# Attention heads and gated-linear-attention chunks moved between the quarters of their projections, in two stages of a four-layer kernel

## The chip, the cores and the metric

One core of one Trainium2 chip runs the whole program. The metric is device time in microseconds (us), as a median over runs. The engines are named as in the profile: PE is TensorE's matmul, PEld its weight load, DVE is VectorE, ACT is ScalarE, POOL is GpSimd, SP is the engine that issues nearly all loads.

## The reference, cut to what matters

A sequence of 256 tokens, 1024 wide, passes through two blocks of two layers each. The change touches the mixers of the first block:

```python
mkv = (mem @ w_mem_kv[l]).reshape(B, MEM_LEN, 2, MEM_HEADS, MEM_HEAD_DIM)
# layer 0: gated linear attention (GLA), 4 heads, chunks of 64 tokens
h = x @ a_w_in[0]                     # q, k (4x96), v, r (4x192), gate root (16), qm (4x64)
g_pre = h[..., A_G0:A_G1] @ a_w_gate2[0] + a_b_gate[0]
log_a = log_sigmoid(g_pre) / 16
o = _gla(q, k, v, log_a)              # chunks: masked q k^T v, and a state carried from chunk to chunk
o = o * rsqrt(mean(square(o), -1) + 1e-6) * a_norm_g[0]
mix = silu(r) * o
# layer 1: dilated attention, 6 slots of 128, three groups of queries on the same keys and values
mix = _dilated_attention(qd, shared_k, shared_v)
# both: attention of 4 heads to 256 memory rows, then the output product and the layer norm
mo = _mem_attn(qm, mkv[:, :, 0], mkv[:, :, 1])
x = _layer_norm(DN_ALPHA * x + concatenate([mix, mo]) @ w_out[l], ...)
f = _peer(x, ...)                     # 128 x 128 experts, the long part of each layer
```

The three dilated groups are softmaxes weighted by their own sums, which is one softmax over the three masked score rows side by side; its numerators are added over the groups before they meet the values.

## The kernel before

**Projections.** `project_all` runs a list of projections on every engine. Each has two units (the two halves of the 1024 input rows, g = 0 and 1), and unit i of the list is projection i // 2, half i % 2. SP loads a unit in two halves into a ring of 7 buffers. ACT rounds a half (`round_half`), DVE subtracts to get the rest (`rest_half`), and TensorE multiplies three times per product (`mm3`): high by high, high by rest, rest by high. In a unit with g = 0, TensorE goes input chunk by input chunk over all outputs of the projection; with g = 1 it finishes one output after the other. After each quarter `project_pe` calls `beside(unit, quarter)`; ACT and DVE call it in `project_all` after rounding each half of the next unit. At the end of an odd unit `project_out` copies the outputs out of PSUM, in turn on DVE and ACT, and then `hooks` for that unit run. A projection's outputs lie in banks 0 to 3 or 4 to 7 in turn (`base` None), or from a given `base`. At g = 0 TensorE takes the banks of all outputs before its first matmul: `take` waits until the last reader of the bank is done, `give` names that reader.

**Heads.** Attention is a list of jobs, one for a head and 128 tokens. In step s, job s gets its scores on TensorE, job s - 1 its row maximum on DVE (`add_max` with the mask), job s - 2 its exponentials on ACT, job s - 3 is turned on TensorE, job s - 4 is copied from PSUM (even jobs on DVE, odd ones on ACT), job s - 5 meets its values on TensorE and job s - 6 is scaled and stored by DVE. All three engines walk the same steps, each in its own order. Before the change these steps run by themselves, after all projections (`join` waits for every engine), with their banks dealt out in turn over seven (`bank_plan`), and with filler matmuls between them (`busy`, tile `gk`, bank 7). For the dilated jobs (scores 384 wide for tokens 0 to 127, 768 for the rest) POOL adds the second and third group to the first (`heads_pool`), and TensorE turns the sum.

**First layer.** After seven projections (Aq, Ak, Ag, Av, Aw, Ar, As) with the gate's chain of small operations in hooks come eight memory jobs, then the chunks: products inside the chunks (`intra`), turned keys (`kend`), three states, the rows (`gla`, 128 tokens each), the head norms with one root for each 128 tokens, then `out_turn` and `out_pe` of the output product in four quarters of 256 input columns.

**Dilated layer.** After ten projections come twelve dilated and eight memory jobs, and then the output product.

**The same arrangement elsewhere.** The last attention stage ("stick") already has its steps between the quarters of its projections, with the projections in banks 0 to 3 and the steps in banks 4 to 7, and its last steps between the halves of the output product.

## Time and profile before

| | us |
|---|---|
| runs shown | 2862.23, 2867.27, 2860.39 (median 2862.23) |
| profiled execution, its own time | 2862.17 |
| its span, first to last instruction | 2860.2 |
| mean granted TensorE clock | 0.982 of full |
| first layer, first projection matmul to end of output product | 47.91 to 184.53 |
| dilated layer, end of projections to end of output product | 1115.50 to 1178.23 |

The program is one long chain of stages on one core. Busy shares over the whole span say little of a stage; the stretch that matters is read by windows and by the timeline. In a timeline row the number in brackets is idle time of that engine before the row. A matmul's record is longer than the pace at which matmuls follow each other, so paces are taken from start to start. A plain fp32 matmul leaves two records, which the xcount includes.

### The profile page before, as it was taken

The page shows a single profiled execution, that of the slowest core. Times are in us where ns is not written, and L with a number is a line of the kernel's source. Part 1 is how long each engine was busy: PE and PEld are TensorE (multiplying, and loading weights), DVE is VectorE, ACT ScalarE, POOL GpSimd, SP SyncE. Part 2 cuts the span into 40 slices and gives each one's busy share as a digit, 9 for nine tenths or more (in the row PEclk, how much of TensorE's full clock was granted, in tenths as well). Part 3 has the DMA queues.
Part 4 walks back from the last instruction along what each step waited for, and adds up shares of the span by engine and source line. Part 5 has one row for each costly group of instructions (what it writes and reads, how often), then busy time and mean ns, then how long its engine had stood idle before and what let it go on. Part 6 is the DMA issues. An engine that isn't in the chain of part 4 may idle for free.

```text
span 2860.2 us, 43908 instructions
## 1 busy us (share of the span) xinstructions
PE 2742.7 (96%) x17298; PEld 2407.5 (84%) x17298; DVE 2001.6 (70%) x3889; ACT 1345.8 (47%) x2188; POOL 302.5 (11%) x162
## 2 busy tenths in 40 slices
PE   7999999999999999999999999999999899898997
PEld 7779999998888888799999988888777678786776
DVE  4676988985555655679889755556657759656588
ACT  3423554444445534435454444455235357453465
POOL 0003950000000001049400000000110000000000
PEclk9999999999999999999999999999999999999999
DMA  5344554555665644445544555656421359532586
GB/s 191 113 136 126 177 175 157 155 164 184 195 194 191 223 147 133 142 133 177 170 157 157 167 185 195 194 192 210 125 89 24 125 193 355 185 99 68 174 296 226
DMA packets 175116, 479.04 MB, mean 167 GB/s; under 512 B 27184, under 2 KB 43456, under 8 KB 174912
## 3 DMA queue, kind: packets, MB, share of 16 engines
q1 hardware_dynamic: 171808, 473.29, 50.5%
q10 hardware_dynamic: 3104, 2.95, 0.3%
q8 instruction: 138, 2.26, 0.3%
q14 instruction: 66, 0.54, 0.1%
HBM read 474.61 MB, written 1.57 MB: 166 GB/s over the span
## 4 chain that ended last, share of the span: by engine, by line
PE 87%; DVE 7%; ACT 3%; POOL 2%; issue 1%; DMA 0%; SPq 0%; DVEq 0%; ACTq 0%; POOLq 0%
PE ps L134 86%; POOL ring_rest L154 2%; PE ps L137 2%; DVE spl L154 1%; DVE big L162 1%; ACT big L140 1%; DVE st L178 1%; ACT whi L140 1%; DVE big L154 1%; DVE xb L162 1%; DVE st L162 0%; ACT spl L140 0%; DVE xr L154 0%; POOL big L154 0%; DVE grouped L154 0%
## 5 line engine op out<-in xcount | busy, mean ns | idle before, releaser
L140 ACT ACTIVATE whi<-ring 128x1024 fp32r<-128x1024 f32 x512 | 542.5, 1060 | 686.6 <-PE ps L134 684.7
L134 PE MATMUL ps<-xr,whi 128*128 128x256 f32 x4096 | 750.4, 285 | 11.1 <-POOL ring_rest L154 10.7
L154 DVE TENSOR_TENSOR ring_rest<-ring,whi 128x1024 fp32r<-128x1024 f32 x412 | 503.5, 1222 | 318.1 <-ACT whi L140 318.1
L134 PEld LDWEIGHTS ps<-xr,whi 128*128 128x128 f32 x4096 | 640.4, 193 | 14.0 <-DVE big L184 8.6
L134 PE MATMUL ps<-whi,Ar 128*128 128x512 f32 x2048 | 631.1, 389 | 4.5 <-DVE Ar L154 4.5
L134 PE MATMUL ps<-xr,ring_rest 128*128 128x256 f32 x2048 | 580.8, 284 | 0.0
L154 DVE TENSOR_TENSOR spl<-ring,spl 128x1024 fp32r<-128x1024 f32 (+3 forms) x384 | 435.3, 1163 | 124.9 <-ACT spl L140 115.8
L134 PEld LDWEIGHTS ps<-whi,Ar 128*128 128x128 f32 x2048 | 384.5, 188 | 84.4 <-DVE Ar L154 4.9
L140 ACT ACTIVATE spl<-ring 128x1024 fp32r<-128x1024 f32 (+3 forms) x384 | 373.4, 1008 | 94.5 <-PE ps L134 75.6
L134 PE MATMUL ps<-ring_rest,Ar 128*128 128x512 f32 x1024 | 398.4, 389 | 0.0
L134 PEld LDWEIGHTS ps<-xr,ring_rest 128*128 128x128 f32 x2048 | 394.4, 193 | 0.0
L140 ACT ACTIVATE big<-ps 128x256 f32<-128x256 f32 (+25 forms) x417 | 153.6, 368 | 366.0 <-PE ps L134 249.8
L154 POOL TENSOR_TENSOR ring_rest<-ring,whi 128x1024 fp32r<-128x1024 f32 x100 | 267.2, 2689 | 263.4 <-ACT whi L140 262.8
L134 PE MATMUL ps<-xr,spl 128*128 128x256 f32 (+2 forms) x2184 | 276.6, 287 | 14.3 <-DVE xr L154 9.7
L134 PEld LDWEIGHTS ps<-xr,spl 128*128 128x128 f32 (+2 forms) x2184 | 267.3, 190 | 19.3 <-DVE xr L154 12.4
L134 PE MATMUL ps<-spl,xr 128*128 128x512 f32 (+2 forms) x1152 | 250.5, 375 | 10.4 <-DVE xr L154 5.3
L134 PEld LDWEIGHTS ps<-spl,xr 128*128 128x128 f32 x1152 | 203.1, 196 | 48.2 <-DVE spl L154 6.4
L134 PE MATMUL ps<-spl,grouped 128*128 128x512 f32 x960 | 234.1, 400 | 4.9 <-DVE spl L154 4.4
L134 PEld LDWEIGHTS ps<-ring_rest,Ar 128*128 128x128 f32 x1024 | 192.3, 188 | 40.0
L134 PEld LDWEIGHTS ps<-spl,grouped 128*128 128x128 f32 x960 | 180.1, 191 | 43.7 <-DVE spl L154 5.4
L154 DVE TENSOR_TENSOR big<-big 128x8 f32<-128x8 f32 (+18 forms) x145 | 158.6, 1125 | 5.8 <-POOL big L154 3.7
L151 DVE COPY big<-ps 128x256 f32<-128x256 f32 (+7 forms) x134 | 55.8, 421 | 147.4 <-PE ps L134 141.0
(127 smaller groups left out, 2488.6 us busy)
## 6 DMA issues: line engine op xcount, KB each, us to landing
ring<-in_peer_u_dram SPq DMA_DIRECT2D x256, 512.0 KB, 3.5
ring<-in_peer_v_dram SPq DMA_DIRECT2D x256, 512.0 KB, 3.5
ring<-in_moe_gate_up_dram SPq DMA_DIRECT2D x128, 512.0 KB, 5.0
ring<-in_moe_w_down_dram SPq DMA_DIRECT2D x64, 512.0 KB, 5.1
ring<-in_peer_w_q_dram SPq DMA_DIRECT2D x32, 512.0 KB, 4.6
ring<-in_sb_w_in_dram SPq DMA_DIRECT2D x24, 512.0 KB, 4.8
ring<-in_ab_w_in_dram SPq DMA_DIRECT2D x20, 512.0 KB, 6.0
ring<-in_w_out_dram SPq DMA_DIRECT2D x16, 512.0 KB, 4.7
```

The lines of the kernel that those rows point to most:

```text
L134: return self.e.matmul(o, l, r, start=start, stop=stop)
L137: return self.e.transpose(o, i, ident)
L140: return self.e.activation(o, i, f, **k)
L151: return self.e.tensor_copy(o, i)
L154: return self.e.tensor_tensor(o, a, b, op)
L162: return self.e.scalar_tensor_tensor(out=o, in0=a, scalar=s, in1=b, op0=op0, op1=op1)
L178: return self.e.bn_stats(o, i)
```

## The change

The steps of the heads become functions of their own (`heads_step_pe`, `_dve`, `_act`) and run in `beside` between quarters of the projections: 14 steps in units 3 to 9 of the first layer, and 20 of 26 steps in units 4 to 17 of the dilated one, the other six between the halves of its output product (`dil_finish`). Banks are fixed: scores in 4 and 5, turned in 6, values in 7, projections in 0 to 3 (but the second of the dilated layer, and the first of the first, in 4 and up). `join`s and fillers go, but for six fillers in the first layer. The sum over the dilated groups moves from POOL to TensorE: a product with the identity for each group, accumulated in PSUM. The first layer projects the gates first; chunk work goes into hooks 10 to 12, squares move from DVE to ACT, and one root serves all 256 tokens. The dilated layer projects keys, values and memory queries first, then queries by head, for which a load takes four separate pieces of 128 columns (512 bytes a row). The rest of the diff moves code without changing it, or hands names through.

```diff
+        def beside_plan(jobs):
+
+            plan = {}
+            for s in range(len(jobs)):
+                plan["scores", s] = 4 if total(jobs[s]) > 512 else 4 + s % 2
+                plan["turn", s], plan["out", s] = 6, 7
+            return plan
+
...
-                    if j.get("sum"):
-                        pe.wait_ge(*gps.at((name, "sum", i)))
...
+            if 0 <= s - 5 < len(jobs):
+                i = s - 5
+                j, b = jobs[i], plan["out", i]
+                take(pe, b)
+                pe.wait_ge(*(vec if i % 2 == 0 else acted).at((name, "copied", i)))
...
+                groups = j.get("sum", 1)
+                w = total(j) // groups
+                for k in range((w + 127) // 128):
+                    n = min(128, w - k * 128)
+                    o = bank(b)[0:n, k * 128:(k + 1) * 128]
+                    for g in range(groups if groups > 1 else 0):
+                        ins = pe.matmul(o, Pm(i)[:, g * w + k * 128:g * w + k * 128 + n], ident, g == 0, g == groups - 1)
+                    if groups == 1:
+                        ins = tp(pe, o, Pm(i)[:, k * 128:k * 128 + n])
+                ins.then_inc(*psum.next((name, "turned", i)))
...
+            if s < len(jobs):
+                j, b = jobs[s], plan["scores", s]
+                nb = (total(j) + 511) // 512
+                take(pe, b, nb)
...
+                for i in range(b, b + nb):
+                    give(pe, i, (vec, (name, "max", s)) if j["mask"] is not None else (acted, (name, "exp", s)))
 
...
+            elif stage == "dil":
+                dil_finish(e, name, following)
...
-        projA = [projection("Aq", WA, 0, 384, [Tcols(96 * h, 96, qA[:, h, :]) for h in range(4)]),
+        projA = [projection("Ag", WA, 2304, 272, [Tcols(0, 128, gT, 16), Tcols(16, 128, qmT[:, 0, :]),
+                                                  Tcols(144, 128, qmT[:, 1, :])]),
...
+        for p_, b_ in zip(projA, (4, 0, 0, 0, 2, 0, 2)):
+            p_["base"] = b_
...
-        HOOKS_A = {"V": {2: [tables_dve], 6: [gate_dve], 8: [log_dve], 9: [scan_dve], 11: [qk_dve], 13: [kend_dve]},
...
+        def squares_act(act, t):
+
+            for h in range(4):
+                act.wait_ge(*psum.at(("gla", t, h // 2)))
+                act.activation(mix[:, t, 192 * h:192 * h + 192], bank(gla_bank(t, h // 2))[:, 192 * (h % 2):192 * (h % 2) + 192], ACT.Square,
+                               accum_out=ss[:, 4 * t + h:4 * t + h + 1]).then_inc(*acted.next(("squares", t)))
+
+        def silu_act(act, k):
+            need(act, stored(projA, (5 + k, 0), (5 + k, 1)))
+            d = slice(512 * k, 512 + 256 * k)
+            act.activation(rA[:, :, d], rA[:, :, d], ACT.Silu).then_inc(*acted.next(("silu", k)))
+
...
+        A_AT = [(3, 0), (3, 2), (4, 0), (4, 2), (5, 0), (5, 2), (6, 0), (6, 2), (7, 0), (7, 2), (8, 0), (8, 2), (9, 0), (9, 2)]
+
+        def gla_beside(e):
+            def beside(i, k):
+                if (i, k) in A_AT:
+                    heads_step(e, "memA", jobsA, planA, buffersA, A_AT.index((i, k)))
+            return beside
+
+        HOOKS_A = {"V": {0: [tables_dve], 2: [gate_dve, log_dve], 4: [scan_dve], 6: [qk_dve], 8: [kend_dve], 10: [chunks_dve],
+                         11: [lambda e: states_dve(e, 0), lambda e: states_dve(e, 1)], 12: [lambda e: states_dve(e, 2)]},
+                   "A": {1: [tables_act], 2: [abs_act], 3: [log_act], 5: [exp_act], 7: [end_act], 12: [lambda e: silu_act(e, 0)]},
+                   "P": {2: [gate_pe], 10: [chunks_pe], 11: [lambda e: states_pe(e, 0), lambda e: states_pe(e, 1)],
+                         12: [lambda e: states_pe(e, 2), lambda e: rows_pe(e, 0)]},
+                   "S": {11: [lambda e: load(e, "norm_g", lambda r: [(r[:, 0:768], io["a_norm_g"].to_broadcast([128, 768]))],
+                                             (vec, ("r", 1)))]}}
+
...
+            if e.name == "P":
+                rows_pe(e, 1)
+            elif e.name == "A":
+                squares_act(e, 0)
+                silu_act(e, 1)
+                round_unit(e, (name, 0))
+                squares_act(e, 1)
+            elif e.name == "V":
+                gains_dve(e, 0)
+                rest_unit(e, (name, 0))
+                gains_dve(e, 1)
+            if e.name in "PAV":
+                turn_rows(0)
+                out_both(e, name, 0, following)
+            if e.name == "V":
+                for t in range(2):
+                    e.wait_ge(*acted.at(("squares", t)))
+                step(e, e.tensor_scalar(ss, ss, 1.0 / 192.0, HEAD_EPS, ALU.mult, ALU.add))
+                rsqrt(e, rn, ss, wk)
                 for h in range(4):
                     d = slice(192 * h, 192 * h + 192)
-                    dve.stt(mix[:, t, d], mix[:, t, d], rn[:, h:h + 1], rA[:, t, d], ALU.mult, ALU.mult).then_inc(
-                        *vec.next(("mixA", t, h)))
-            vec.close(("end", "gla"))
-
-        def gla_pool(pool):
-            join(pool, "A")
-            for i in range(2):
-                pool.memset(aT[i], 0.0).then_inc(*gps.next(("zero", i)))
-            gps.close(("end", "gla"))
-
-        def gla_finish(e, name, following):
-
+                    for t in range(2):
+                        o = bank(gla_bank(t, h // 2))[:, 192 * (h % 2):192 * (h % 2) + 192]
+                        e.stt(mix[:, t, d], o, rn[:, 4 * t + h:4 * t + h + 1], rA[:, t, d], ALU.mult, ALU.mult).then_inc(
+                            *vec.next(("mixA", t, h)))
...
+                busy(e, 6)
             if e.name in "PAV":
-                join(e, "gla")
...
-        out_units("wo1", io["w_out"][1], 0, 1, 2, 3)
+        out_units("wo1", io["w_out"][1], 3, 0, 1, 2)
...
+        QB = [(h, g) for h in range(6) for g in range(3)]
+        projB = [projection("Bk", WK, 0, 512, [Tcols(128 * i, 128, kD[:, i, :]) for i in range(4)]),
+                 projection("Bl", WK, 512, 256, [Tcols(128 * i, 128, kD[:, 4 + i, :]) for i in range(2)]
+                            + [Tcols(256 + 128 * i, 128, qmT1[:, i, :]) for i in range(2)], [(WB, 2304, 256)]),
+                 projection("Bv", WK, 768, 512, Nrows(0, 512, lambda t: vD[:, t, 0:512]))]
         for n0 in range(0, 18, 4):
-            k = min(4, 18 - n0)
-            projB.append(projection(f"Bq{n0}", WB, 128 * n0, 128 * k, [Tcols(128 * i, 128, qD[:, n0 + i, :]) for i in range(k)]))
-        projB += [projection("Bm", WB, 2304, 256, [Tcols(128 * i, 128, qmT1[:, i, :]) for i in range(2)]),
-                  projection("Bk", WK, 0, 512, [Tcols(128 * i, 128, kD[:, i, :]) for i in range(4)]),
-                  projection("Bl", WK, 512, 256, [Tcols(128 * i, 128, kD[:, 4 + i, :]) for i in range(2)]),
-                  projection("Bv", WK, 768, 512, Nrows(0, 512, lambda t: vD[:, t, 0:512])),
-                  projection("Bw", WK, 1280, 256, Nrows(0, 256, lambda t: vD[:, t, 512:768]))]
-
-        jobsB = []
+            at_q = [6 * g + h for h, g in QB[n0:n0 + 4]]
+            projB.append(projection(f"Bq{n0}", WB, 128 * at_q[0], 128,
+                                    [Tcols(128 * i, 128, qD[:, c, :]) for i, c in enumerate(at_q)],
+                                    [(WB, 128 * c, 128) for c in at_q[1:]]))
+        projB.append(projection("Bw", WK, 1280, 256, Nrows(0, 256, lambda t: vD[:, t, 512:768])))
+        for n, p_ in enumerate(projB):
+            p_["base"] = 4 * (n == 1)
+
...
+        planB = beside_plan(jobsB)
+        buffersB = heads_buffers(8192, 768)
+
+        B_AT = [(4, 0), (4, 2), (5, 0), (5, 2), (6, 0), (6, 2), (7, 0), (7, 2), (8, 0), (8, 2), (10, 0), (10, 2),
+                (12, 0), (12, 2), (13, 0), (13, 2), (14, 0), (15, 0), (16, 0), (17, 0)]
+
+        def dil_beside(e):
+            def beside(i, k):
+                if (i, k) == B_AT[0] and e.name == "P":
+                    e.wait_ge(arrival("kv1"), 16)
+                if (i, k) in B_AT:
+                    heads_step(e, "dil", jobsB, planB, buffersB, B_AT.index((i, k)))
+            return beside
 
...
-            busy(pe, 4)
-            join(pe, "B")
-            pe.wait_ge(arrival("kv1"), 16)
-            heads_pe(pe, "dil", jobsB, planB, PTB, PmB, 2, 0)
-            psum.close(("end", "dil"))
...
-        def dil_pool(pool):
-            gps.close(("end", "B"))
-            join(pool, "B")
-            heads_pool(pool, "dil", jobsB, PmB)
-            gps.close(("end", "dil"))
+            project_all(dve, projB, "x2", 2, None, dil_beside(dve))
+
+        def dil_finish(e, name, following):
+
+            def advance(s):
+                heads_step(e, "dil", jobsB, planB, buffersB, s)
+
+            def turn_rows(k, job):
+                out_turn(e, name, k, [(vec, ("dil", "stored", job))])
+            if e.name == "A":
+                round_unit(e, (name, 0))
+            elif e.name == "V":
+                rest_unit(e, (name, 0))
+            if e.name in "PAV":
+                advance(20)
+                turn_rows(0, 7)
+                out_half(e, name, 0, 0, following)
+                advance(21)
+                out_half(e, name, 0, 1, following)
+                turn_rows(1, 11)
+                advance(22)
+                out_half(e, name, 1, 0, following)
+                advance(23)
+                turn_rows(2, 15)
+                out_half(e, name, 1, 1, following)
+                advance(24)
+                out_half(e, name, 2, 0, following)
+                advance(25)
+                out_half(e, name, 2, 1, following)
+                turn_rows(3, 19)
+                out_both(e, name, 3, following)
 
 
         pr = scr[:, 0:5680].rearrange("p (t n) -> p t n", t=2)
```

## Rows read from the trace of the kernel before

**Rows 1.** Page, part 1: busy time, share of the span, instructions by engine

```profile
PE 2742.7 (96%) x17298; PEld 2407.5 (84%) x17298; DVE 2001.6 (70%) x3889; ACT 1345.8 (47%) x2188; POOL 302.5 (11%) x162
```

**Rows 2.** Windows: busy us of each engine, granted clock (PEclk), DMA share, GB/s

```profile
115.00:120.00 5.00, 3.47 (x19) 3.48 (x20) 2.07 (x3) 2.32 (x4) 2.48 (x3) 0.73 0.41 133
1185.00:1190.00 5.00, 4.70 (x24) 3.77 (x25) 5.00 (x13) 1.19 (x2) 0.00 (x0) 0.66 0.00 0
2580.00:2585.00 5.00, 1.94 (x9) 1.64 (x10) 5.00 (x8) 3.90 (x7) 0.00 (x0) 1.00 0.57 112
```

**Rows 3.** Windows: first layer projections to output product; dilated heads to output product

```profile
47.91:184.53 136.62, 132.03 (x792) 111.15 (x793) 90.35 (x182) 55.25 (x87) 5.17 (x6) 0.98 0.41 133
1115.50:1156.35 40.85, 37.14 (x228) 28.61 (x227) 28.25 (x106) 23.10 (x59) 14.15 (x24) 1.00 0.02 9
```

**Rows 4.** Windows of the tile gk (filler matmuls) in the same two stages

```profile
120.90:164.80 43.90, 18.16 (x64) 5.68 (x64) 0.00 (x0) 0.00 (x0) 1.00 0.18 61
1115.40:1153.90 38.50, 5.47 (x20) 1.90 (x20) 0.00 (x0) 0.00 (x0) 1.00 0.02 9
```

**Rows 5.** Timeline of TensorE, first layer: start, us, operation [idle before <-releaser]

```profile
116.53 4.63 PE L134 MATMUL ps<-spl,xr 128*128 128x256 f32 x24 [2.33 <-DVE spl L154]
...
153.53 4.08 PE L134 MATMUL ps<-big 128*128 128x192 f32 x24
...
168.09 16.60 PE L134 MATMUL ps<-spl,xr 128*128 128x512 f32 x72 [0.81 <-DVE xr L154]
```

**Rows 6.** Timeline of VectorE, then of ScalarE, first layer

```profile
155.80 0.17 DVE L159 TENSOR_SCALAR st<-st 128x4 f32<-128x4 f32 x1
...
158.38 1.41 DVE L162 SCALAR_TENSOR_TENSOR big<-big,st 128x192 f32<-128x192 f32 x4
...
125.65 0.47 ACT L140 ACTIVATE big<-ps,st 128x256 f32<-128x256 f32 x1 [4.52 <-DVE st L158]
126.03 0.19 ACT L140 ACTIVATION_READ_ACCUMULATOR big<-ps,st 128x1 f32 x1
```

**Rows 7.** Timeline of TensorE, dilated heads

```profile
1116.81 0.83 PE L134 MATMUL ps<-big 128*128 128x128 f32 x6
1117.47 0.59 PE L134 MATMUL ps<-gk 128*128 128x512 f16 x2
1117.90 1.46 PE L134 MATMUL ps<-big 128*128 128x256 f32 x6
...
1131.09 0.41 PE L137 MATMUL ps<-cst,big 128*128 128x128 f32 x2 [0.33 <-POOL big L154]
1131.34 1.06 PE L134 MATMUL ps<-big 128*128 128x128 f32 x8
...
1134.58 0.41 PE L137 MATMUL ps<-cst,big 128*128 128x128 f32 x2 [0.32 <-POOL big L154]
...
1156.35 22.04 PE L134 MATMUL ps<-spl,xr 128*128 128x512 f32 x96 [0.76 <-DVE xr L154]
```

**Rows 8.** Timeline of VectorE, then of ScalarE, dilated heads

```profile
1130.35 0.96 DVE L171 CUSTOM_DVE_ANT_0 big<-ps,big 128x768 f32<-128x768 f32 x1 [0.37 <-PE ps L134]
...
1118.68 1.28 ACT L140 ACT_TABLE_LOAD   x1 [2.60 <-DVE st L158]
1119.97 0.61 ACT L140 ACTIVATE big<-big,st 128x384 f32<-128x384 f32 x1
```

**Rows 9.** Timelines in the stick stage: TensorE, ScalarE, VectorE

```profile
2512.30 1.70 PE L134 MATMUL ps<-xr,spl 128*128 128x256 f32 x12
2514.68 1.66 PE L134 MATMUL ps<-xr,spl 128*128 128x256 f32 x12 [0.68 <-ACT big L140]
...
2583.06 2.98 PE L134 MATMUL ps<-spl,xr 128*128 128x512 f32 x12 [3.19 <-DVE xr L154]
...
2514.32 1.05 ACT L140 ACTIVATE spl<-ring 128x1024 fp32r<-128x1024 f32 x1
...
2515.40 1.23 DVE L154 TENSOR_TENSOR spl<-ring,spl 128x1024 fp32r<-128x1024 f32 x1 [1.77 <-ACT spl L140]
```

More of the change, by code:

```diff
@@ L572, in heads_pe @@
-                if 0 <= s - 3 < len(jobs):
-                    i = s - 3
-                    j, b = jobs[i], plan["turn", i]
-                    take(pe, b)
-                    pe.wait_ge(*acted.at((name, "exp", i)))
-                    if j.get("sum"):
-                        pe.wait_ge(*gps.at((name, "sum", i)))
-                    w = total(j) // j.get("sum", 1)
-                    for k in range((w + 127) // 128):
-                        n = min(128, w - k * 128)
-                        ins = tp(pe, bank(b)[0:n, k * 128:(k + 1) * 128], Pm(i)[:, k * 128:k * 128 + n])
-                    ins.then_inc(*psum.next((name, "turned", i)))
-                    give(pe, b, (vec if i % 2 == 0 else acted, (name, "copied", i)))
@@ L585, in heads_pe @@
-                if s < len(jobs):
-                    j, b = jobs[s], plan["scores", s]
-                    nb = (total(j) + 511) // 512
-                    take(pe, b, nb)
-                    need(pe, j.get("after", ()))
-                    at = 0
-                    qs = j["q"] if isinstance(j["q"], list) else [j["q"]] * len(j["keys"])
-                    for q, k in zip(qs, j["keys"]):
-                        n = k.shape[1]
-                        ins = pe.matmul(bank(b, nb)[:, at:at + n], q, k, True, True)
-                        at += n
-                    ins.then_inc(*psum.next((name, "scores", s)))
-                    for i in range(b, b + nb):
-                        give(pe, i, (vec, (name, "max", s)) if j["mask"] is not None else (acted, (name, "exp", s)))
+                heads_step_pe(pe, name, jobs, plan, PT, Pm, s)
@@ L640, in heads_act @@
         def heads_act(act, name, jobs, plan, PT, Pm, Sm, stat):
             for s in range(len(jobs) + 6):
-                if 0 <= s - 4 < len(jobs) and (s - 4) % 2 == 1:
-                    i = s - 4
-                    w = total(jobs[i]) // jobs[i].get("sum", 1)
-                    n, nk = min(128, w), (w + 127) // 128
-                    act.wait_ge(*psum.at((name, "turned", i)))
-                    if i >= 2:
-                        act.wait_ge(*psum.at((name, "out", i - 2)))
-                    act.activation(PT(i)[0:n, 0:nk * 128], bank(plan["turn", i])[0:n, 0:nk * 128], ACT.Copy).then_inc(
-                        *acted.next((name, "copied", i)))
@@ L662, in heads_pool @@
[L662 to L671 removed]
+                heads_step_act(act, name, jobs, plan, PT, Pm, Sm, stat, s)
@@ new lines, in heads_step_act @@
+        def heads_step_act(act, name, jobs, plan, PT, Pm, Sm, stat, s):
+            if 0 <= s - 4 < len(jobs) and (s - 4) % 2 == 1:
+                i = s - 4
+                w = total(jobs[i]) // jobs[i].get("sum", 1)
+                n, nk = min(128, w), (w + 127) // 128
+                act.wait_ge(*psum.at((name, "turned", i)))
+                if i >= 2:
+                    act.wait_ge(*psum.at((name, "out", i - 2)))
+                act.activation(PT(i)[0:n, 0:nk * 128], bank(plan["turn", i])[0:n, 0:nk * 128], ACT.Copy).then_inc(
+                    *acted.next((name, "copied", i)))
+            if 0 <= s - 2 < len(jobs):
+                i = s - 2
+                j, s4, tot = jobs[i], stat(i), total(jobs[i])
+                if i >= 3:
+                    act.wait_ge(*psum.at((name, "turned", i - 3)))
+                act.wait_ge(*vec.at((name, "neg", i)))
+                src = Sm(i) if j["mask"] is not None else bank(plan["scores", i], (tot + 511) // 512)
+                act.activation(Pm(i)[:, 0:tot], src[:, 0:tot], ACT.Exp, bias=s4[:, 1:2],
+                               scale=1.0 if j["mask"] is not None else j["scale"], accum_out=s4[:, 2:3]).then_inc(
+                                   *acted.next((name, "exp", i)))
@@ L1001, in tables_act, with gate_bank @@
             act.activation(csn[:, :, :, :], ang4, ACT.Sin).then_inc(*acted.next("sines"))
+        def gate_bank(h):
+            return bank(4 + h // 2)[0:96, 256 * (h % 2):256 * (h % 2) + 256]
         def gate_pe(pe):
@@ L1063, in end_pool @@
             for i in range(2):
+                pool.memset(aT[i], 0.0).then_inc(*gps.next(("zero", i)))
+            for i in range(2):
                 step(pool, pool.memset(z5[i][:, :, 1 - i, :], 0.0))
```

411 lines of the change are left out of this document (196 added, 215 removed).

## The prediction

> **What bounds the kernel now.** The page comes first: TensorE is busy 96% of the span, the others far less [rows 1], so what counts is how long TensorE works and where it waits. The windows then give the two stages that the change touches [rows 3]. From the first layer's first projection to the end of its output product TensorE is busy 132.03 of 136.62 us; in the dilated heads, from the last projection to the output product, 37.14 of 40.85. That looks full. The windows of the tile gk say that it isn't: 64 filler matmuls lie in the one stage and 20 in the other [rows 4], at 0.215 us each by start to start (1117.47 to 1117.90, two of them) [rows 7]. So the first stage holds 13.8 us of fillers and 4.6 us of idle time, and 118.2 us of real work; the second 4.3 and 3.7, and 32.8 of real work. The timeline shows that the steps between are packed: a pair of dilated jobs takes 3.49 us, from the turning at 1131.09 to that at 1134.58, of which TensorE idles only 0.33 for POOL [rows 7]. Interleaving can win back fillers and idle time, 18.4 and 8.0 us at most. Real work only moves.
>
> **First layer, gain.** I follow TensorE to the end of the last projection, X. Real work that stays behind X: the second rows (from 153.53, 24 records, 3.8 us), the output product (72 records in 16.60, so 5.5 a quarter, 22.1 in all) [rows 5], and 16 turnings at 0.125 (two in 0.25, 1131.09 to 1131.34) [rows 7], 1.9 rounded down. Before X lie 118.2 - 3.8 - 22.1 - 1.9 = 90.4. The start comes 0.6 earlier, at 47.3, since the first unit is narrower (an estimate). Stalls before X: Ak takes the same banks as Aq, and the copy of Aq's last output waits behind the first maximum on DVE, 1.0. In unit 6 the step needs DVE's store, behind ACT's two exponentials of 96x1024 (`exp_act`), a rounding and a rest: 2.3 net. Tables in hook 0: 0.3. X is 47.3 + 90.4 + 3.6 = 141.3.
>
> Behind X, ACT has in order squares 0 (4 x 0.5 as an estimate from 0.47 and 0.19 for 256 columns [rows 6]), silu 1 (0.6), two roundings of 1024 at 1.0 [rows 9], squares 1 (2.0) and the turned copy (0.6). It ends at X + 6.3, DVE's rest of it at X + 7.0, and only then can the output product start. TensorE's own work ends at X + 4.3, so it idles 2.7. The first quarter ends at X + 12.6, six fillers at X + 13.9. DVE reaches the root at X + 9.8; one root takes 2.6 (155.80 to 158.38), eight products with 192 columns 8 x 0.36 [rows 6], so the heads end at X + 15.3. The turned rest for the next quarter waits for them in DVE's queue until X + 16.1. Three quarters more: X + 32.7 = 174.0, against 184.5. The gain is 10.5 us, with 15 and 6 as bounds (no stall before X and a short one behind; twice these).
>
> **Dilated layer, the sum on TensorE.** For each block of 128 keys, one turning becomes three fp32 products with the identity. Six jobs have one block and six have two: 54 products for 18 turnings. The nearest row has the same shape, 128 columns against a 128x128 weight: three in 0.66 (1116.81 to 1117.47) [rows 7], 0.22 each. 54 x 0.22 - 18 x 0.125 = +9.7 us on the engine that is full. POOL's part (0.33 idle a pair) is already in the 3.7 that goes. By this alone the stage's gain of 8.0 is spent. The low bound is a product at a turning's pace, +4.5.
>
> **Bank waits between projections.** Before, consecutive projections use banks 0-3 and 4-7 in turn. After, four boundaries (units 7|8, 9|10, 11|12, 15|16) take the banks just written, with no step behind the last output. The stick stage shows the price: idle 0.68 at 2514.68 for ACT's copy [rows 9]. 4 x 0.68 = 2.7.
>
> **Waits inside a step.** The new plan has one bank (6) for turned and one (7) for values. So TensorE's values of job s - 5 need DVE's store of job s - 6, and its turning needs the copy of s - 4: both belong to the same step s. Dilated scores all use bank 4, and need the maximum of job s - 1, again step s. Where the step is the first of an even unit, DVE reaches it late. In the stick stage the unit ends at 2513.99, ACT copies, rounds from 2514.32, DVE subtracts from 2515.40, and its step can begin 2.6 us after the unit's end [rows 9]. With the store, the value bank is free at 2.85. TensorE is there at 0.68 + 1.46 (12 matmuls) = 2.15: 0.7 lost at steps 8, 10 and 12. Step 10 also waits for the 0.96 maximum [rows 8], 0.8 more. Step 4 loses 0.9 behind a 512-wide copy; step 16 (two outputs a chunk, so only 0.73 of cover) 1.2; step 18, 0.5. Sum 5.5, with 0 as the low bound (the stick stage has such steps and no wait, but with two banks) and 9 as the high one.
>
> **The finish.** After the last projection DVE has the whole first output unit to subtract (2 x 1.2, behind ACT) before step 20, and `out` of job 15 waits for its store of job 14: 4.0 idle. Then 2.3 of work, then 1.35 until the turned rest. The stick stage idles 3.19 in this place [rows 9], with an emptier step. Later, step 22 waits for a store behind the turned rest, 1.6, and the last quarter turns with nothing between, 1.35. Sum 8.3, bounds 4.5 and 10.
>
> Sum for the dilated layer: -8.0 + 9.7 + 2.7 + 5.5 + 8.3 = +18.2. Hidden at no cost: the rearranged loads. A half comes in four pieces instead of one, but TensorE takes over 2.9 us for a half and DMA is idle in most of the stage (share 0.02 in the heads) [rows 3]. If 512-byte rows moved at half pace, a half would still land in time. Weight rounding and rests are the same elements. Copies alternate as before.
>
> **The total.** +18.2 - 10.5 = +7.7 us. The profiled execution took 2862.17, the median of the runs is 2862.23, so they agree. I predict 2870.
>
> One rule was weighed. A table switch costs ACT 1.28 us, and the next activation starts as it ends (1118.68, then 1119.97) [rows 8]. The Trainium skill ("ScalarE: Activation LUTs", What ACT_TABLE_LOAD costs) puts a switch at about 2.66 us with its drain; this trace doesn't show the drain. Its section on table sets says that cheap functions are in every set. By its price three extra switches would give 8.0 us instead of the 3.8 below.
>
> **Rivals.**
> (a) *The same-step waits don't bite*: not slower. DVE and ACT are busy only 28.25 and 23.10 of 40.85 us in the heads [rows 3] and catch up; the 5.5 vanish and the finish costs 4.5 as in the stick stage. Dilated +8.9, total -1.6: 2861. It speaks for it that the stick stage runs its steps without stalls; against it, its steps don't need the same step of DVE. It decides if stalls inside the dilated units stay under 1 us in all.
> (b) *Faster*: (a) holds and the first layer reaches its bound of -15 and the sums run at the turning's pace: 8.9 - 5.2 - 15 = -11, 2851.
> (c) *The clock falls.* Without fillers, waits may drop TensorE to 1.2 GHz. An idle time of 2.33 us before 116.53 went with a mean clock of 0.73 over 5 us, and the layer norm's window at 1185 shows 0.66; yet 3.19 us in the stick stage went with 1.00 [rows 2, 5, 9]. A drop of 0.3 over 5 us costs 1.5 us. Before, the dilated heads run at 1.00 [rows 3]; four or five drops there give +7: 2877.
> (d) *Table switches*: if Square isn't in Silu's set, ACT switches three times more at X, 3.8 us by the row: 2874.
> (e) *The change does little*: loads in 512-byte rows arrive late and TensorE waits for them in the ten query units, 0.5 us each: 2875.
>
> **How the numbers follow.** Forecast 0.40 (2863 to 2877), (a) 0.25, (b) 0.15, (c) 0.12, (d) 0.05, (e) 0.03. About 0.3% (8.6 us) is what a measurement of this kernel can tell from no change: 2853.6 to 2870.8. The forecast lies just inside, so half of its 0.40 counts as slower: slower 0.20 + 0.20 = 0.40; same 0.20 + nearly all of (a) and a little of (b), 0.43; faster 0.17. The range runs from (b) to just over (c), 2852 to 2880.
>
> **What would show it.** Right: fillers gone from both stages; the first layer's product ends near 174 at similar start; 108 records of fp32 matmul against the identity, about 0.11 apart; TensorE rows with idle before them of 0.5 to 1.5 at the even units of the dilated layer, released by DVE; an idle of 4 us behind its last projection; from its first projection to the end of the output product some 18 us more than before. Wrong: a dilated stage that grows by less than 10 us, a first layer that gains under 6, or a TensorE clock below 0.9 over either.

## The result and the profile after

The changed kernel takes 2871.94 us (median of 11 runs, 2869.81 to 2882.79) against 2862.34 of the kernel before (11 runs): ratio 1.003, 95% interval 1.0017 to 1.0044. That is 9.6 us slower where +7.7 and 2870 were forecast. The profiled execution spans 2870.9 us; before, 2860.2.

The page after, busy time and share of the span. TensorE is busy 2.2 us less in a span that is 10.7 longer, and GpSimd's sums are gone:

```profile
PE 2740.5 (95%) x17310; PEld 2410.9 (84%) x17310; DVE 1994.0 (69%) x3868; ACT 1345.0 (47%) x2197; POOL 286.8 (10%) x138
```

Windows after: first projection to output product of the first layer (136.62 long before, [rows 3]), then the dilated layer from the first turning of the layer norm ahead of it to that of the norm behind it:

```profile
46.12:170.75 124.63, 118.82 (x734) 103.83 (x735) 83.28 (x165) 55.61 (x100) 3.69 (x6) 0.99 0.47 149
...
1005.87:1194.77 188.90, 169.03 (x1154) 149.99 (x1154) 96.52 (x212) 67.17 (x118) 0.00 (x0) 0.98 0.44 135
```

and the second stretch before:

```profile
1018.98:1185.30 166.32, 158.83 (x1084) 140.42 (x1084) 98.10 (x216) 68.49 (x122) 14.15 (x24) 1.00 0.45 153
```

So the first layer gives 12.0 and the dilated layer costs 22.6. TensorE was busy for all but 7.5 us of the latter before, and is idle for 19.9 after. Who it waits for there (us in total, times, longest):

```profile
PE ps L134 <- DVE big L158: 9.6, 8, 4.1
PE ps L134 <- DVE xr L154: 3.7, 3, 1.5
PE ps L137 <- DVE xb L162: 2.3, 2, 1.8
PE ps L134 <- ACT big L140: 2.0, 3, 0.7
PE ps L137 <- DVE big L151: 0.8, 1, 0.8
PE ps L134 <- issue: 0.5, 1, 0.5
PE ps L134 <- DVE st L171: 0.4, 1, 0.4
```

L158 is the store of a head's output, L151 the copy of a turned block, L171 the maximum, L140 the copy of a projection's last output: each of these four is an instruction that frees a PSUM bank. L154 is the rest of turned rows, L162 the layer norm, and "issue" a wait for which the profile names no releaser. VectorE is busy for 96.52 of the 188.90 us, so it isn't short of time; its instructions come late. Before, the list was GpSimd's sum 2.9, the norm's 2.3 and 1.5 for turned rests.

TensorE in the dilated layer after. The first two rows are the boundary of two projections and, right behind it, a wait of 0.54 us for the value bank, at the start of a unit of even number (compare [rows 9] of the stick stage). Then come the maximum, the steps 16 and 20, the turned rest, and step 22:

```profile
1067.05 1.66 PE L134 MATMUL ps<-xr,spl 128*128 128x256 f32 x12 [0.68 <-ACT big L140]
1069.25 0.66 PE L134 MATMUL ps<-big 128*128 128x64 f32 x4 [0.54 <-DVE big L158]
...
1086.91 0.94 PE L134 MATMUL ps<-big 128*128 128x128 f32 x6 [0.38 <-DVE st L171]
...
1124.76 0.71 PE L134 MATMUL ps<-big 128*128 128x128 f32 x4 [1.26 <-DVE big L158]
...
1150.67 1.22 PE L134 MATMUL ps<-big 128*128 128x128 f32 x4 [4.07 <-DVE big L158]
...
1156.81 3.00 PE L134 MATMUL ps<-spl,xr 128*128 128x512 f32 x12 [1.50 <-DVE xr L154]
...
1165.55 0.71 PE L134 MATMUL ps<-big 128*128 128x128 f32 x4 [1.67 <-DVE big L158]
```

Behind the idle 4.07 us the granted clock is halved. The same two products (four records) take 1.22 us at 1150.67 and 0.71 at 1165.55. Windows after:

```profile
1145.00:1150.00 5.00, 1.59 (x13) 1.38 (x11) 2.01 (x2) 2.87 (x5) 0.00 (x0) 0.91 0.00 0
1150.00:1155.00 5.00, 4.33 (x20) 4.24 (x20) 1.90 (x7) 0.00 (x0) 0.00 (x0) 0.50 0.58 210
1155.00:1160.00 5.00, 3.50 (x18) 2.71 (x17) 3.19 (x5) 3.68 (x6) 0.00 (x0) 0.91 0.07 24
```

TensorE in the first layer after: the boundary of two projections, the step of unit 6, the head products behind the last projection (they start at X), the turned rest, the six fillers, the turned rest again. Compare [rows 5]:

```profile
72.30 1.63 PE L134 MATMUL ps<-xr,spl 128*96 128x256 f32 x12 [1.00 <-DVE big L151]
...
89.97 0.66 PE L134 MATMUL ps<-big 128*128 128x64 f32 x4 [0.53 <-DVE big L158]
...
137.26 4.08 PE L134 MATMUL ps<-big 128*128 128x192 f32 x24
141.18 0.60 PE L137 MATMUL ps<-cst,big 128*128 128x128 f32 x4
143.47 5.72 PE L134 MATMUL ps<-spl,xr 128*128 128x512 f32 x24 [1.69 <-DVE xr L154]
150.90 1.47 PE L134 MATMUL ps<-gk 128*128 128x512 f16 x6 [1.71 <-DVE big L162]
152.21 1.47 PE L137 MATMUL ps<-cst,big 128*128 128x128 f32 x12
154.31 5.95 PE L134 MATMUL ps<-spl,xr 128*128 128x512 f32 x25 [0.63 <-DVE xr L154]
```

### The profile page after: what moved, and what is told of

Its sections match the earlier page's. It is cut to its first block, busy times and chain, and to the rows that moved or that the text cites. A ratio compares the mean times of both kernels' runs of the same rounds, so it can differ in the third digit from the quotient of the medians.

```text
span 2870.9 us, 43899 instructions
## 1 busy us (share of the span) xinstructions
PE 2740.5 (95%) x17310; PEld 2410.9 (84%) x17310; DVE 1994.0 (69%) x3868; ACT 1345.0 (47%) x2197; POOL 286.8 (10%) x138
## 4 chain that ended last, share of the span: by engine, by line
PE 87%; DVE 7%; ACT 3%; POOL 2%; issue 1%; DMA 0%; ACTq 0%; SPq 0%; DVEq 0%
PE ps L134 86%; DVE spl L154 2%; POOL ring_rest L154 2%; PE ps L137 2%; DVE big L162 1%; DVE st L178 1%; ACT spl L140 1%; ACT big L140 1%; ACT whi L140 1%; DVE xb L162 1%; DVE st L162 0%; DVE big L154 0%; DVE xr L154 0%; DVE grouped L154 0%; ACT L140 0%
## 5 line engine op out<-in xcount | busy, mean ns | idle before, releaser
L140 ACT ACTIVATE whi<-ring 128x1024 fp32r<-128x1024 f32 x512 | 542.5, 1060 | 687.4 <-PE ps L134 687.3
L134 PE MATMUL ps<-xr,whi 128*128 128x256 f32 x4096 | 751.5, 286 | 11.1 <-POOL ring_rest L154 10.7
L154 DVE TENSOR_TENSOR ring_rest<-ring,whi 128x1024 fp32r<-128x1024 f32 x412 | 503.5, 1223 | 318.0 <-ACT whi L140 318.0
L154 DVE TENSOR_TENSOR spl<-ring,spl 128x1024 fp32r<-128x1024 f32 (+3 forms) x380 | 436.8, 1173 | 130.0 <-ACT spl L140 120.9
L140 ACT ACTIVATE spl<-ring 128x1024 fp32r<-128x1024 f32 (+3 forms) x380 | 374.8, 1016 | 88.7 <-PE ps L134 67.6
L154 POOL TENSOR_TENSOR ring_rest<-ring,whi 128x1024 fp32r<-128x1024 f32 x100 | 267.2, 2689 | 1040.5 <-ACT whi L140 1039.9
L140 ACT ACTIVATE big<-ps 128x256 f32<-128x256 f32 (+24 forms) x421 | 154.3, 367 | 384.4 <-PE ps L134 263.7
L134 PE MATMUL ps<-xr,spl 128*128 128x256 f32 (+2 forms) x2184 | 284.2, 289 | 16.9 <-DVE xr L154 9.8
L134 PEld LDWEIGHTS ps<-xr,spl 128*128 128x128 f32 (+2 forms) x2184 | 269.5, 191 | 27.2 <-DVE xr L154 12.6
L154 DVE TENSOR_TENSOR big<-big 128x64 f32<-128x64 f32 (+16 forms) x143 | 156.7, 1127 | 5.8 <-POOL big L154 3.7
L151 DVE COPY big<-ps 128x256 f32<-128x256 f32 (+7 forms) x134 | 55.7, 420 | 142.8 <-PE ps L134 137.5
```

The costliest lines, as they stand in the source:

```text
L134: return self.e.matmul(o, l, r, start=start, stop=stop)
L140: return self.e.activation(o, i, f, **k)
L151: return self.e.tensor_copy(o, i)
L154: return self.e.tensor_tensor(o, a, b, op)
```

## The experiments

Each was timed beside the kernel before, whose median was 2861.74 to 2862.92. "Stage" is the dilated layer between the two norms' first turnings: 166.32 us before, 188.90 after. The differences against the changed kernel are between medians, and each carries a few us of noise: the code behind the dilated layer took 1674.0 to 1685.2 us in the profiled executions of the 11 kernels in which it is the same (all but the two that wait for banks one at a time). So stages are read beside medians. A stage with the same code differs too, by some 1.5 us, and the traces show why: the same wait is followed by a lower granted clock in one execution and not in another. The first layer of the changed kernel took 137.0 to 137.1 us from first turning to first turning where the clock fell behind a wait of 3.43 us at its start, and 135.5 and 135.6 in the two executions (those of "Sums on GpSimd" and "The finish in another order") where it stayed at 1.00.

**First layer alone.** The dilated layer and its finish are those of before.

> The first layer as in the changed kernel, the dilated layer and its output product as before. Theory (the two layers are independent terms: first layer -12 to -14 by the trace after, dilated +22.8): 2862.3 - 13.1 = 2849, and the dilated layer's first to last event takes 159.3 us again. By the prediction's term of -10.5 it would be 2852. Rival (the gain of the first layer is lost in the stage behind it, because its loads or its rounding meet something else): 2856 to 2862.

2853.32 us (2849.27 to 2859.09), ratio 0.9959 (0.9944 to 0.9973), so -9.6. The dilated stage took 167.7, the first layer the same 137.04 from norm to norm as in the changed kernel (149.44 before). The 1.4 us by which this dilated stage is longer than before's are a fall of the clock at its start (0.93 and 0.73 in the windows from 1005 to 1015, where before's trace has 1.00). So the layers are independent. The median is nearer to the forecast's -10.5 than to the trace's -12 to -13, but the interval, -16 to -8, holds both.

**Dilated layer alone.**

> The dilated layer and its output product as in the changed kernel, the first layer as before. If the layers are independent terms: by the stages in the two traces (dilated 166.3 to 188.9 us, first turning to first turning of the norms around it) 2862.9 + 22.6 = 2885.5; by the medians (changed kernel less the one with the first layer alone, 18.6) 2881.5; by the prediction's +18.2, 2881. The dilated stage itself: 188 to 190 us. Rival (part of the dilated layer's loss is caused by the new first layer): under 2877.

2884.14 us (2883.52 to 2894.83), ratio 1.0073 (1.0057 to 1.0089): +22.4, its stage 191.9 (the clock fell at its start too, to 0.66 from 1020 to 1025, and stayed at 0.50 for a second window behind the wait of 4.07). This is nearer to the trace's 22.6 than to the forecast's 18.2, though the interval, 16 to 25, holds both. The rival's 2877 lies below every run: no part of the loss comes from the new first layer.

**Sums on GpSimd.** The edit, shortened:

```diff
-                    for g in range(groups if groups > 1 else 0):
-                        ins = pe.matmul(o, Pm(i)[...], ident, g == 0, g == groups - 1)
+                    ins = tp(pe, bank(b)[0:n, ...], Pm(i)[:, k * 128:k * 128 + n])   # behind gps (name, "sum", i)
...
+            heads_pool(pool, "dil", jobsB, buffersB[1])
```

> The changed kernel, but GpSimd adds the three groups again and TensorE turns once, instead of three products with the identity a block. Theory (the identity products cost the 9.7 of the prediction, and a step now lasts 6 to 8 us, so GpSimd's two additions are done before TensorE's turning): 2871.9 - 9.7 = 2862, no wait of TensorE on GpSimd inside the projections. Rival 1 (GpSimd is late as it was before, 2.9 us of waits in all, and more in the finish where steps are short): 2865 to 2867. Rival 2 (the identity products only filled time in which TensorE would wait for VectorE anyway, so the same-step waits grow as they go): 2867 to 2872.

2862.12 us, ratio 0.9998 (0.9987 to 1.0008): 9.8 less than the changed kernel, stage 180.69, that is 8.2 less. TensorE never waits for GpSimd, and the other waits stay nearly as they were (those for the maximum come to 1.0 us in place of 0.4). The theory holds. The products with the identity are one of the two large costs of the change; the late copies and stores of the next run cost about as much, and the two can't be told apart by these times.

**Copies and stores a step earlier.** VectorE and ScalarE free banks 6 and 7 at the end of the step in which TensorE filled them. The edit is shown as if made in place; the run uses a second version of the two functions, in the dilated layer alone:

```diff
-            if 0 <= s - 6 < len(jobs):          # first in VectorE's step
-                i = s - 6
...
+            if 0 <= s - 5 < len(jobs):          # last in VectorE's step
+                i = s - 5
...
-            if 0 <= s - 4 < len(jobs) and (s - 4) % 2 == 0:
+            if 0 <= s - 3 < len(jobs) and (s - 3) % 2 == 0:
```

> The changed kernel, but in the dilated layer VectorE and ScalarE copy a turned job and store an output at the end of the step in which TensorE makes it, not in the next step; the same instructions otherwise. Theory (the 4.6 us of same-step waits and the 4.1 us behind the last projection come from banks 6 and 7 being freed one step late, and the clock fall behind the latter costs 2.6): 2871.9 - 4.6 - 4.1 - 2.6 = 2860.6. Rival (VectorE is late because of the weight rests ahead of its step, whichever instruction comes first, and now waits for TensorE at each step's end, so rests come later): the waits change place, 2869 to 2880.

2862.73 us, ratio 0.9997 (0.9987 to 1.0008): -9.2, stage 181.37. All waits on L158 are gone and the stage is 7.5 us shorter, with no rest late. But behind the last projection something else is next. TensorE in that kernel, and the clock behind it:

```profile
1083.09 0.94 PE L134 MATMUL ps<-big 128*128 128x128 f32 x6 [0.66 <-DVE st L171]
...
1144.86 0.66 PE L137 MATMUL ps<-cst,big 128*128 128x128 f32 x4 [2.96 <-DVE st L171]
1147.02 5.46 PE L134 MATMUL ps<-spl,xr 128*128 128x512 f32 x12 [1.50 <-DVE xr L154]
```
```profile
1145.00:1150.00 5.00, 3.50 (x11) 2.73 (x11) 2.24 (x4) 3.40 (x5) 0.00 (x0) 0.62 0.58 190
```

The turning of the first rows uses bank 4, which the maximum of job 19 frees late (2.96 us in place of 4.07), and the clock still falls. So 3.0 us of wait and most of the clock's price stayed that the theory's -11.3 took as gone. Against them stand the waits for stores at steps 22 and 24, 1.67 and 0.42, which the theory hadn't counted and which went too.

**Fillers in the 4.07 us wait.** The edit, shortened:

```diff
+            if e.name == "P":                   # ahead of advance(20)
+                take(e, 3)
+                for _ in range(16):
+                    e.matmul(bank(3), gk[:, 0, 0:128], gk[...], True, True)
```

> The changed kernel, with 16 filler matmuls (some 3.5 us) on the free bank 3 in front of step 20, where TensorE now idles 4.07 us behind the last projection. Nothing else moves. Theory (the idle time drops the granted clock to about 0.5 for some 5 us behind it, at a cost of 2.5 us over and above the wait): idle falls to about 0.6, the clock stays at 1.00, 2871.9 - 2.5 = 2869.4. Rival (the clock fall costs nothing, since what follows waits for VectorE and ScalarE anyway): 2872, with longer waits behind. If the fillers delay step 20: 2873.

2868.11 us (2866.55 to 2869.6), ratio 1.0014 (1.0005 to 1.0023): -3.8, stage 186.83 (-2.1). Step 20, and the windows at the same place:

```profile
1149.14 0.71 PE L134 MATMUL ps<-big 128*128 128x128 f32 x4 [0.61 <-DVE big L158]
```
```profile
1145.00:1150.00 5.00, 4.39 (x24) 2.25 (x23) 3.54 (x6) 2.87 (x5) 0.00 (x0) 1.00 0.13 45
1150.00:1155.00 5.00, 3.50 (x23) 2.98 (x22) 2.62 (x7) 3.33 (x6) 0.00 (x0) 1.00 0.45 168
```

Step 20 waits for the same store, but the clock holds at full speed and the work from there to the next wait, the one of 1.50 us, takes 2.49 us (1149.14 to 1151.63) instead of 4.64 (1150.67 to 1155.31). The clock's fall cost 2.15 us, apart from the wait. All 12 runs of this kernel (2866.55 to 2869.6) are shorter than every one of the 11 of the changed kernel, the shortest of which took 2869.81.

**No fillers in the first layer's finish** (`busy(e, 6)` removed).

> The changed kernel without the six fillers in the first layer's finish. They sit on bank 7, which VectorE's last head product but one frees, so TensorE, and with it the turning of the first normed rows, waits 1.71 us for a bank that only the fillers need. Theory (the turning can start at the fourth head product instead of behind the fillers, 149.8 instead of 152.2): the product and all that follows 2.4 us earlier, 2871.9 - 2.4 = 2869.5. Rival 1 (the fillers pay: without them the clock falls in the product and costs 2 or more): 2871 to 2875. Rival 2 (the turning waits for VectorE's products all the same): 2871, with an idle of 2.5 to 3 us before the turning.

2870.17 us (2868.21 to 2873.01), ratio 1.0025 (1.0016 to 1.0035): -1.8. TensorE there:

```profile
152.27 1.93 PE L137 MATMUL ps<-cst,big 128*128 128x128 f32 x12 [0.82 <-DVE big L162]
154.40 5.93 PE L134 MATMUL ps<-spl,xr 128*128 128x512 f32 x25 [0.20 <-DVE xr L154]
```

From X to the end of the product TensorE takes 31.3 us here (139.52 to 170.83) and 33.5 in the changed kernel (137.26 to 170.75); the two later kernels without these fillers take 31.3 as well. That is 2.2 us, nearly the theory's 2.4. The whole first layer is only 1.2 shorter in this execution (135.80 from turning to turning), because its first 120 matmuls, behind the wait of 3.43 us, ran longer at the lower clock: 16.81 us, against 15.88 in the changed kernel's trace. The median's -1.8 alone would prove nothing, since the two intervals overlap. Rival 1 falls: from X to the end of the product the clock stayed at 1.00.

**Sums on GpSimd and early copies together.**

> Both edits of the second group of runs together: sums on GpSimd, and copies and stores at the end of TensorE's own step. If they are independent: 2871.9 - 9.8 - 9.2 = 2852.9. Rival (with copies at the end of a step, VectorE and ScalarE stand behind TensorE's turning, which stands behind GpSimd's sum; a late sum now holds up the weight rests as well): 2857 to 2865, with waits of TensorE on GpSimd or on rests.

2858.11 us (2856.82 to 2865.89), ratio 0.9983 (0.9972 to 0.9994): -13.8 from the changed kernel, where independent edits would give -19.0. The stage is 177.3, 11.6 less, where the stages of the two runs would give 15.7. The longest waits of TensorE there:

```profile
PE ps L137 <- DVE st L171: 4.1, 1, 4.1
PE ps L134 <- DVE xr L154: 3.7, 3, 1.5
PE ps L134 <- DVE st L171: 3.1, 4, 1.3
```

The time lies in the rival's range, but the rival's cause isn't there: neither GpSimd nor a rest is late. With neither identity products nor stores ahead of it, TensorE comes to the next bank sooner: dilated scores all use bank 4, and the maximum that frees it is still in the same step. These waits were 0.7 and 3.0 with the identity products in place. So 3.5 of the 5 lost us are waits that the dear products had covered; a wait of 0.8 for a reciprocal (L168) is new.

**The finish in another order.**

```diff
+            if e.name in "PAV":
+                turn_rows(0, 7, 3)              # bank 3, ahead of rounding and step 20
...
                 advance(24)
+                turn_rows(3, 19)
                 out_half(e, name, 2, 0, following)
-                advance(25)
                 out_half(e, name, 2, 1, following)
-                turn_rows(3, 19)
                 out_both(e, name, 3, following)
```

> The same, with another order in the dilated layer's finish: the rows of the memory heads are turned right behind the last projection, on the free bank 3 and ahead of the rounding of the first output unit and of step 20, and the last rows right behind step 24, ahead of the third quarter's products. Theory (both 1.50 us waits for a turned rest go, since other work lies between; step 20 waits no more for bank 4; what is left is the wait for the first output unit's rests, some 2 us, too short for the clock to fall): pool_and_early - 1.5 - 1.5 - 1.5 - 1 = some 2847. Rival (the rests of the output unit, behind ScalarE's rounding, end 4 us after the last projection whatever the order, and the clock falls as before): only the last 1.5 go, 2851.

2854.15 us (2850.64 to 2857.35), ratio 0.9965 (0.9953 to 0.9978): 4.0 less than the kernel above, stage 170.13 (-7.2, of which 1.4 is a fall of the clock at the start of the stage above that this execution doesn't have). Both the theory's 2847 and the rival's 2851 lie below the median. Both 1.50 us waits are gone; what is left:

```profile
1140.58 4.57 PE L134 MATMUL ps<-spl,xr 128*128 128x512 f32 x12 [2.27 <-DVE spl L154]
```
```profile
1140.00:1145.00 5.00, 4.42 (x13) 3.51 (x14) 4.16 (x9) 3.01 (x7) 2.60 (x4) 0.66 0.58 181
```

The 2.27 us wait for the output unit's rests comes out as expected, but "too short for the clock to fall" was wrong: 0.66, and twelve matmuls that take 2.98 at full clock take 4.57. The four waits for the maximum, 3.1 us in all, stay as well.

**Banks waited for one at a time.**

```diff
-                for n, o in outs:
-                    take(pe, out_bank(p, pr, n))
                 for i in range(4):
                     for n, o in outs:
+                        if i == 0:
+                            take(pe, out_bank(p, pr, n))
```

> The changed kernel, but a projection waits for each of its banks only ahead of that bank's first product, not for all of them ahead of the first. It is the same in every stage. Theory (the waits of 0.68 at the boundaries of the dilated layer are for the last output's bank alone, which is needed 9 products, over 1.0 us, later): three of the four go, with the drain behind each, 2871.9 - 2.4 = 2869.5; a little less if the same-step waits behind them grow. Rival (those waits only hide the next one: VectorE's step comes as late as before, so the stop moves to the step): 2871.5, with the waits at steps 8, 10 and 12 longer by 0.7 each.

2874.86 us (2868.1 to 2877.87), ratio 1.0028 (1.0016 to 1.004): no gain. TensorE idles 19.8 us in the stage, as in the changed kernel (19.9); the stage took 189.8, with one more fall of the clock (0.81 and 0.85 from 1080 to 1090) than the changed kernel's 188.9. The boundary rows are gone, and step 8 (steps 10 and 12 alike) shows where they went:

```profile
1065.23 0.66 PE L134 MATMUL ps<-big 128*128 128x64 f32 x4 [1.44 <-DVE big L158]
```

0.68 + 0.54 became 1.44. The rival is right in its mechanism: the two waits are one lateness, VectorE's, read at two places.

**All of it.** The reordered finish, the maximum too in its own step, banks one at a time, ten fillers on bank 2 in the 2.27 us wait, none in the first layer's finish; sums on GpSimd and early copies as above.

> The reordered kernel with, besides, the maximum in VectorE's own step as well, banks waited for one at a time, ten fillers (2.2 us) on the free bank 2 where it idles 2.27 us ahead of the first output quarter, and no fillers in the first layer's finish. Theory (each removes the waits that the trace shows: maxima 3.1, boundaries 2.0, clock 1.3, first finish 1.7, some 8 in all): 2854.2 - 8 = 2846, the dilated stage at 164, as before or less. Rival (with the maximum in its own step VectorE waits for TensorE four times a step, its weight rests come late, and what is gained at the banks is lost at the rests): 2852 to 2858.

2843.62 us (2841.79 to 2845.99), ratio 0.993 (0.9917 to 0.9942): 18.7 less than the kernel before, 28.3 less than the changed one. The stage takes 163.4, under before's 166.3, and all of TensorE's waits in it, the two norms' apart, are:

```profile
PE ps L134 <- DVE big L151: 2.2, 3, 1.3
PE ps L134 <- DVE xr L154: 0.7, 1, 0.7
PE ps L137 <- DVE big L158: 0.4, 1, 0.4
```
```profile
1126.83 2.32 PE L134 MATMUL ps<-gk 128*128 128x512 f16 x10
1129.27 3.00 PE L134 MATMUL ps<-spl,xr 128*128 128x512 f32 x12
```

The boundary waits could not be had alone (the run before this one); with the step's other waits gone, they can. Several edits went in together here, so what each is worth isn't shown.

**First layer alone, without its fillers.**

> The first layer as in the changed kernel without the six fillers of its finish, the dilated layer as before the change. Theory (independent terms): 2853.3 - 1.7 = 2851.6. Rival (the fillers' absence costs as much as it gives): 2853.3. Against all_together it tells which of the two versions is the best one: by the theories all_together by 5 us, by its rival first_no_fill by 3.

2852.02 us (2845.39 to 2857.41), ratio 0.9952 (0.9936 to 0.9968). 1.3 less than with the fillers; the two intervals overlap, but the first layer's 134.8 us from turning to turning, against 137.0, shows the 2.2 of the run without fillers again. The version with both layers changed is 8.4 us better.

## Why the prediction came out right, term by term

The forecast of +7.7 stands against +9.6 (interval 4.9 to 12.6), because both layers were signed and sized nearly right. That it came so near is in part luck, since two misses partly cancel: by the traces the first layer gave 1.5 more than its -10.5, and the dilated layer cost 4.4 more than its +18.2.

- **First layer, -10.5:** -12.0 from projection to product by the trace, -9.6 by the medians. The boundary Aq/Ak cost 1.0, as forecast. The step of unit 6 cost 0.53, not 2.3; the trace shows the shorter wait, and no run its cause. X came at 137.26 rather than 141.3: 1.2 of it is a start at 46.12 instead of 47.3, 1.8 are shorter stalls, and 1.1 is less work than the sum's 90.4. The sum took TensorE's busy time before as work, and 24 matmuls at 116.53 took 4.63 us there at a granted clock of 0.73, where 24 at full clock take 3.1; after, that wait and that fall of the clock are gone. Behind X the rest came after 1.69, not 2.7: the terms listed for ScalarE add up to 7.2, not to the sum's 6.3, but ScalarE was done at X + 5.3, since the first squares began before X and each took 0.3, not 0.5. One wait wasn't foreseen: the fillers, costed as six short matmuls, wait 1.71 on bank 7. The product ended at X + 33.5 (X + 32.7 forecast).
- **Identity products, +9.7:** 8.2 by the stage, 9.8 by the medians. The 108 records are there, and twelve of them (six products) take 1.34 from start to start, the 0.22 each of the sum.
- **Boundaries, +2.7:** three of 0.68 and one of 0.52, for which the profile names no releaser, 2.6. The one-at-a-time run shows that they are not a term of their own: without them the three same-step waits of 0.54 take 0.9 more each.
- **Same-step waits, +5.5:** steps 4 to 18 in the places named, 0.77, 0.54, 0.54 + 0.38, 0.54, 1.26 and 0.52, in all 4.6. Rival (a) falls. The early copies show the mechanism: with them the waits for stores are gone.
- **Finish, +8.3:** 4.07, 1.50, 1.67, 0.42 and 1.50, in all 9.2; the 0.42 had not been counted. The early copies and the new order removed each by its named cause, except that the maximum of bank 4 stood behind the store, and that 2.27 for the output unit's rests stayed.
- **The clock:** the step that failed. It was put into rival (c) alone, four or five falls at 1.5 each, and into the forecast at nothing, on the strength of the 3.19 us in the stick stage [rows 9] with 1.00 [rows 2]. In the dilated stage there was one fall, behind the longest wait, of 2.15 us by the filler run. The forecast named that wait, and one row at full clock was no ground for costing it at nothing beside the two rows of 0.73 and 0.66. That row was one outcome of two: behind the same wait of 3.19 us the clock fell in six of the 13 profiled executions (last section).
- **Not in the sum:** with the products at the rows' price, -8.0 + 9.7 + 2.6 + 4.6 + 9.2 + 2.15 is 20.3, and 22.6 was measured. Part of the other 2.3 can be read off the rows: twelve projection matmuls with the pipeline running start 0.123 apart (24 in 2.96 us), 1.48 in all, but ahead of a wait the row lasts 1.66. A wait so costs some 0.18 more than its idle time. TensorE waits 19 times in the stage after and 10 times before, so by this estimate the nine more cost 1.6. No run isolates it. The last version fits: it waits 7 times, three fewer than before, and -8.0 + 2.6 of waits (3.3 less the norm's usual 0.7) + 2.4 of fillers + 0.7 more at the norm behind it - 0.5 gives -2.8, where -2.9 was measured. Under 1 us stays unexplained.
- **Rivals (d) and (e):** no table switch for Square or Silu beyond those of before (three in the first layer before, three after), and no wait on a load in the dilated projections. At one of the switches after, the activation ahead ends at 55.35, the load runs from 55.37 for 1.28 us, and the next activation starts at 56.66. The Trainium skill ("ScalarE: Activation LUTs", What ACT_TABLE_LOAD costs) gives some 2.66 us for a switch with its drain; this trace shows no drain around the load. The row-gathered loads, 72 of 128 KB, land in 2.7 us (median). The argument for (e) being nothing was misread, though: the DMA share of 0.02 is that of the heads, while the projections, which these loads feed, had 0.57 before (1018.98 to 1117.47).

## What to carry to other kernels

When work is put between the pieces of a saturated engine's queue, list for each step which instruction frees the bank or buffer that it takes, and in which step of the other engine that instruction stands: here a good part of the gain was eaten because store, copy and maximum stood in the same step as the product that needed their bank. Moving store and copy to the end of their own step gave 9.2 us, and all edits together turned +9.6 into -18.7. Remove such waits as a set, since one alone may only move to the next (the boundary waits did), and expect two edits not to add up where one covered the other's wait. Don't buy freedom on an engine with slack (GpSimd) with work on the engine that bounds. And don't price a wait by one trace: whether TensorE's clock falls behind it can differ from execution to execution.

## What the hardware showed that was not expected

- The same wait is followed by full clock in one execution and by half of it in the next. The stick stage idles 3.19 us (3.20 once) behind its last projection in every trace. In 7 of 13 the granted clock over the next 5 us was 1.00, in 6 it was 0.50 to 0.68 (1.2 of 2.4 GHz for most of it), and the twelve matmuls behind the wait took up to 5.46 us instead of 2.98. In 11 of the traces the stage's code is the same: 7 at 1.00 and 4 below. Here are the changed kernel and the one with the first layer alone:

```profile
2594.14 2.98 PE L134 MATMUL ps<-spl,xr 128*128 128x512 f32 x12 [3.19 <-DVE xr L154]
```
```profile
2576.95 5.46 PE L134 MATMUL ps<-spl,xr 128*128 128x512 f32 x12 [3.19 <-DVE xr L154]
```

- Likewise the wait of 3.43 us at the start of the changed first layer: 1.00 behind it in 2 of 11 traces, 0.50 to 0.66 in 9. Behind the dilated layer's last projection, waits of 2.27, 2.96, 4.07 and 4.08 us gave 0.50 to 0.69 in all eight traces without fillers there. So a wait's length does not decide, and none of these runs shows what does. Filling the gap kept 1.00 in both kernels that did so.
- A wait costs TensorE more than its idle time: by the rows some 0.18 us of what counts as busy ahead of it is lost as well (an estimate). Where two waits of 0.68 and 0.54 became one, it was 1.44.
